# Hybrid attention block on one NeuronCore: buffers that TensorE reads begin at multiples of 128 bytes, and the last two down-projections of half the row tiles share one accumulation

## Chip, cores and metric

The kernel runs on one core of one Trainium2 chip. The metric is the device time of one execution in microseconds (us); lower is better. Everything is float32, and the large matrix products are made from three products each of rounded parts (below).

## What is computed

One layer over x of 1024 rows by 1024 columns. The reference, cut to what matters here:

```
h   = rms_norm(x, g_pre_mix)
proj = h @ w_in                              # 1024 x 2824
mix = concat(gated_delta_rule(...), sliding_window_attention(...)) @ w_out
x   = x + rms_norm(mix, g_post_mix)
h   = rms_norm(x, g_pre_ffn)
u   = causal_depthwise_conv(h @ w_up, ffn_conv_w) + ffn_conv_b   # 1024 x 5632
gate, val = split(u, 2)
y   = (gelu(gate) * val) @ w_down            # contraction over 2816
out = x + rms_norm(y, g_post_ffn)
```

## The kernel before

Three stages run one after the other. The **input projection** (0 to 300 us) multiplies row tiles of 128 by the columns of w_in. The **mixer** (to about 605 us) does the delta rule, the attention and the output projection tile by tile. The **channel block** (`ffn_block`, from 605 us to the end) does the up- and down-projection.

**Products.** A float32 operand is kept as two rounded parts, hi and lo, and a product is three matmuls that accumulate in one PSUM bank: hi by hi, hi by lo, lo by hi. These three are called a triple here. Each matmul has a stationary operand of 128 x 128, loaded before it, and a moving one of 128 x 512. Lines 2256 to 2258 are the triple of the up-projection (stationary `f_w_hi`, `f_w_lo`; moving `split`), lines 2274 to 2276 that of the down-projection (stationary `f_y_hi`, `y_lo`; moving `f_w_hi`, `f_w_lo`), 176 to 178 that of the input projection's convolved columns (stationary `slab_w`, moving `split`), 622 to 624 that of its other columns (stationary `p_tile_hi`, `p_tile_lo`; moving `slab_w` for the first group of columns, 8 triples in each of 8 row tiles, then `p_group`), 1777 to 1779 that of the output projection (stationary `m_mix_hi`, `m_mix_lo`; moving `split`).

**Channel block.** The 2816 hidden columns are taken in FG = 11 groups of 256. A step g does the up-projection of group g (4 channel blocks of 128, 16 triples each) and then the down-projection of group g - 1, whose results go to all 8 row tiles, two banks of 512 columns each: 16 banks, two triples each. Four PSUM banks (`sums`) take turns, and VectorE adds each full bank to the running sum `acc` in `h_t` (line 2139). After the last step `down(FG)` does the down-projection of the last group; its y parts lie in a free slot of `f_w_hi` and `f_w_lo`. TensorE may start a bank once the bank of four before it has been added (`s_acc`), and may start `down(FG)` once the low parts of the last y are there (`s_ylo`, line 2151).

**Last y.** For each of two channel blocks: ScalarE's first tap (L2058) and VectorE's two others (L2127), the product with the gelu (L2161, `s_prod`), ScalarE's rounding (L2090, `s_yhi`), VectorE's low part (L2151, `s_ylo`). On VectorE they stand between additions, in an order written out by hand.

**Tail.** For each row tile t: after its two additions ScalarE squares it (L2113), VectorE scales the sum (L2224), GpSimd raises it to -0.5 (L2240), VectorE multiplies by it and the gain (L2174), the residual is added (L1983; on GpSimd for tiles 0 to 5, on VectorE for 6 and 7), and the tile is stored (L2047). VectorE's order is: additions of tile t, then L2174 of tile t - 1, then L2224 of tile t.

**Where buffers begin.** Buffers of a core's memory are handed out one after another, so the start of each is the sum of the sizes before it. Offsets of the starts from a multiple of 128 bytes, before and after the change:

| buffer | role | before | after |
|---|---|---|---|
| `slab_w`, `split`, `stage`, `y_lo` | both | 0 | 0 |
| `table`, `exact`, `p_tile_hi`, `p_tile_lo`, `p_group` | both | 64 | 0 |
| `f_w_hi`, `f_w_lo`, `f_y_hi` | both | 64 | 0 |
| `m_mix_hi`, `m_mix_lo` | stationary | 96 | 0 |

The 64 comes from `conv_taps`, 48 float32 or 192 bytes in each partition. The slices that the triples of the table take are whole multiples of 512 bytes apart, except in `p_group`'s third part.

Of the kernel before, what the change touches and what calls it, by code (L numbers as in the profile page):

```python
# [20 lines left out]
P = 128  # L21
# [3 lines left out]
ALU = mybir.AluOpType  # L25
# [4 lines left out]
D = 1024  # L30
S = 1024
T = S // P
KD = D // P
HALF = 512
# [5 lines left out]
GTAPS, FTAPS = 4, 3  # L40
DFF = 2816
A_CH = 3 * GH * DK
A_TILES = A_CH // P
# [47 lines left out]
NG = 7  # L91
# [4 lines left out]
class Kept:  # L96


    def __init__(self, nc, ctx):
        sb = lambda name, shape, dt=F32: ctx.enter_context(nc.sbuf_tensor(name, shape, dt))  # L100
        sem = lambda name: ctx.enter_context(nc.semaphore(name))

        def under(name, shape, dt=F32):
            with nc.sbuf_tensor(name, shape, dt) as m:
                return m

        self.slab_w = under("slab_w", [P, KD * S], F32R)
        self.h_t = sb("h_t", [P, KD, S])
        self.split = sb("split", [P, 2, KD, S], F32R)
        self.stage = sb("stage", [P, 2, 2 * P * KD])  # L110
        self.x = sb("x_tile", [P, D])
        self.y_lo = under("y_lo", [P, 2, S], F32R)
        self.conv = sb("conv", [P, 2, S])
        self.g_post, self.g_ffn = self.conv[:, 0], self.conv[:, 1]
        self.taps = sb("conv_taps", [P, GTAPS * A_TILES])
        self.g_out = under("g_out", [P, D])
        self.table = sb("table", [P, T_ROPE])
        self.exact = sb("exact", [P, 4, P], F32R)
        self.gates = sb("gates", [P, T, NG, GH])
        self.own_rows = sb("own_rows", [P, T, GH])  # L120
        self.cum_rows = sb("cum_rows", [P, P], F32R)
        self.sums = ctx.enter_context(nc.psum_tensor("sums", [P, 4, HALF], F32))
        self.s_stage = [sem(f"s_stage{n}") for n in range(2)]
        self.s_slab = [sem(f"s_slab{n}") for n in range(2)]
        self.s_qkv_out = [sem(f"s_qkv_out{n}") for n in range(2)]
        self.s_whi, self.s_wlo = sem("s_whi"), sem("s_wlo")
        self.s_pair, self.s_first, self.s_tap = sem("s_pair"), sem("s_first"), sem("s_tap")
        self.s_conv, self.s_silu = sem("s_conv"), sem("s_silu")
# [95 lines left out]
def project(nc, io, kept):  # L224

    SLOTS = 4
    H = GH
    with ExitStack() as ctx:  # L228
        sb = lambda name, shape, dt=F32: ctx.enter_context(nc.sbuf_tensor("p_" + name, shape, dt))
# [19 lines left out]
        power = sb("power", [P, 1])  # L249
# [11 lines left out]
        ps_t = ctx.enter_context(nc.psum_tensor("ps_t", [P, 2, HALF], F32))  # L261
# [8 lines left out]
        s_whi, s_wlo = kept.s_whi, kept.s_wlo  # L270
        s_taps = sem("s_taps")
# [218 lines left out]
        def _(dve):  # L490
# [46 lines left out]
            for c in range(NCH):  # L537
                g, k0, nk = CHUNKS[c]
# [19 lines left out]
            sums = gate_sums.rearrange("p (c t h) -> p c t h", c=2, h=H)  # L558

            dve.wait_ge(s_ps_g, 1)  # L560
            dve.tensor_copy(kept.taps[:], ps_t[:, 0, 0:GTAPS * A_TILES]).then_inc(s_taps, 1)
            dve.wait_ge(s_taps, 1)
            split_lo(dve, kept, 1)
            conv_rest(dve, kept, 0, 0)
# [113 lines left out]
def mix_block(nc, io, kept):  # L678
    project(nc, io, kept)

    with ExitStack() as ctx:
        sb = lambda name, shape, dt=F32: ctx.enter_context(nc.sbuf_tensor("m_" + name, shape, dt))
# [12 lines left out]
        zw = [m.rearrange("p (h c) -> p h c", c=P) for m in (left[:, A_TILES * P:(A_TILES + H) * P], late_zw[:])]  # L695
        row = right[:, 0:ROW]
        o = right[:, ROW:ROW + H * P].rearrange("p (h c) -> p h c", c=P)
        gs = sb("gs", [P, 2, NG, H])
        power = sb("power", [P, 2, H])

        gates, own_rows, cum_rows, exact = kept.gates, kept.own_rows, kept.cum_rows, kept.exact
        row_cum = sb("row_cum", [P, H, P], F32R)

        norm2 = sb("norm2", [P, 2, 2, 2 * H])
        k_pow = sb("k_pow", [P, 2, H])
        k_gate = sb("k_gate", [P, 2, 3, H])
        K_RN, K_LOW, K_NEG = range(3)
        k_out = sb("k_out", [P, 2, H, P])
        b_v = sb("b_v", [P, H, P])
# [9 lines left out]
        resid = sb("resid", [P, H, P])  # L719
        v_new = sb("v_new", [P, H, P])  # L720
        squares = v_new
        o_stat = sb("o_stat", [P, 5, H])
        norm_w = sb("norm_w", [P, P])
        junk = sb("junk", [P, H, P], BF16)

        NB = P // BASE
        SKEW = BASE * (BASE + 1)
        blk = sb("blk", [H * NB, SKEW])
        products = sb("products", [H * NB, (BASE // 2) ** 3])
        half_sum = sb("half_sum", [H * NB, (BASE // 2) ** 2])  # L730

# [3 lines left out]
        v_b = sb("v_b", [P, 2, 2, KVH * HD])  # L735
        probs = sb("probs", [P, PAIRS, P])
        p_t = sb("p_t", [P, PAIRS, P])
        sinks = sb("sinks", [P, PAIRS])
        neg_sinks = sb("neg_sinks", [P, PAIRS])
        c_stat = sb("c_stat", [P, 6, 2 * PAIRS])  # L740

        mix_a = sb("mix_a", [P, H * P])
        mix_c = sb("mix_c", [P, 2, D - H * P])
        mix_hi = sb("mix_hi", [P, KD, P], F32R)
        mix_lo = sb("mix_lo", [P, KD, P], F32R)
        d_stat = sb("d_stat", [P, 6])
        y = sb("y", [P, D])
        table = kept.table
        tab = lambda at: table[:, at:at + P]
        ident = tab(T_ID)  # L750
# [1131 lines left out]
FG = FT // 2  # L1882


def ffn_block(nc, io, kept):
# [4 lines left out]
    with ExitStack() as ctx:  # L1890
# [54 lines left out]
        def n_down(g):  # L1945
            return 3 * g + 2

        LAST_DOWN = n_down(FG) - 2

        def steps(eng, step):  # L1950
            with eng.Fori(1, FG - 1) as g:
# [6 lines left out]
        def dn_w(part, kind):  # L1958
            return (w_hi, w_lo)[part][:, kind].rearrange("p (k n) -> p k n", k=2)

        def y_of(part, last):
            if last:
                return (w_hi, w_lo)[part][:, VALUE].rearrange("p (c s) -> p c s", c=2)
            return (y_hi, y_lo)[part][:]
# [86 lines left out]
        def _(act):  # L2051
# [57 lines left out]
            step(0, False, lead=True)  # L2109
            steps(act, step)  # L2110
            for t in range(T):
                act.wait_ge(s_acc, 16 * (FG - 1) + 2 * t + 2 + 4)
                act.activation(junk[:], acc[:, t], ACT.Square, accum_out=stat[:, 0, t:t + 1]).then_inc(s_sq, 1)  # L2113

        @block.vector
        def _(dve):
# [19 lines left out]
            def accumulate(m, t, half):  # L2136
                dve.wait_ge(s_dn, m + 2)
                cols = acc[:, t, half * HALF:(half + 1) * HALF]
                dve.tensor_tensor(cols, ps_dn[:, (2 * t + half) % 4], cols, ALU.add).then_inc(s_acc, 1)  # L2139

            def step(g, last, lead=False):
                if not lead:
                    split(n_down(g), DOWN, 0)
                for c in range(2):
                    convolve(4 * g + c, c, g * 2 + c)
                split(LAST_DOWN if last else n_gate(g + 1), GATE, 0)
                for c in range(2):
                    convolve(4 * g + 2 + c, 2 + c, g * 2 + (c + FT))
                def low_part(c):
                    dve.wait_ge(s_yhi, 2 * g + c + 1)  # L2150
                    dve.tensor_tensor(y_of(1, last)[:, c], conv[:, 2 + c], y_of(0, last)[:, c].bitcast(F32), ALU.subtract).then_inc(  # L2151
                        s_ylo, 1)

                for j in range(2 * T):
                    if not lead:
                        accumulate(g * 16 + (j - 16), j // 2, j % 2)
                    if j in (3, 6):
                        c = (j - 3) // 3
                        dve.wait_ge(s_gelu, 2 * g + c + 1)
                        dve.wait_ge(s_conv, 4 * g + c + 5)  # L2160
                        dve.tensor_tensor(conv[:, 2 + c], conv[:, c], conv[:, 2 + c], ALU.mult).then_inc(s_prod, 1)  # L2161
                    if j == 9 and not last:
                        split(n_value(g + 1), VALUE, 1)
                    if j in (9, 12) and last:
                        low_part((j - 9) // 3)
                if not last:
                    for c in range(2):
                        low_part(c)

            def finish(t):  # L2170
                if t == T - 1:
# [44 lines left out]
            for t in range(T + 1):  # L2216
                if t < T:
                    for half in range(2):
                        accumulate(16 * (FG - 1) + 2 * t + half, t, half)
                if t >= 1:  # L2220
                    finish(t - 1)
                if t < T:
                    dve.wait_ge(s_sq, t + 1)
                    dve.tensor_scalar(stat[:, 1, t:t + 1], stat[:, 0, t:t + 1], 1.0 / D, EPS, ALU.mult, ALU.add).then_inc(s_ms, 1)  # L2224
# [20 lines left out]
        def _(pe):  # L2245
# [13 lines left out]
                if 1 in halves:  # L2259
                    op.then_inc(s_pair, 1)  # L2260

            def down(g):
                last = isinstance(g, int) and g == FG
                kind = GATE if last else DOWN
                pe.wait_ge(s_wlo, LAST_DOWN if last else n_down(g))
                pe.wait_ge(s_ylo, 2 * g)
                for j in range(2 * T):
                    t, half = j // 2, j % 2
                    pe.wait_ge(s_acc, g * 16 + (j - 15))
                    for k in range(2):  # L2270
                        y = slice(t * P, (t + 1) * P)
                        cols = slice(half * HALF, (half + 1) * HALF)
                        bank = ps_dn[:, j % 4]
                        pe.matmul(bank, y_of(0, last)[:, k, y], dn_w(0, kind)[:, k, cols], start=(k == 0), stop=False)  # L2274
                        pe.matmul(bank, y_of(0, last)[:, k, y], dn_w(1, kind)[:, k, cols], start=False, stop=False)  # L2275
                        op = pe.matmul(bank, y_of(1, last)[:, k, y], dn_w(0, kind)[:, k, cols], start=False, stop=(k == 1))  # L2276
                    op.then_inc(s_dn, 1)

            def ups(g):
                for kind, n in ((GATE, n_gate(g)), (VALUE, n_value(g))):  # L2280
# [3 lines left out]

            def step(g, last):
                ups(g)
                down(g)

            pe.sem_inc(s_dn, 1)
            pe.wait_ge(s_rows, 48)  # L2290
# [16 lines left out]
            for c in range(2):  # L2307
                up(2 + c, VALUE, c)
            steps(pe, step)
            down(FG)  # L2310


# [29 lines left out]
```

## Time and profile before

| | |
|---|---|
| time, 3 runs | 1361.29 us median, 1359.57 to 1361.96 |
| profiled execution | 1361.83 us, span 1360.0 us |
| TensorE busy | 1278.4 us, 94% |
| VectorE, ScalarE, GpSimd busy | 52%, 30%, 11% |
| granted TensorE clock, mean | 0.972 |

The span is what the instruction records cover; the time of an execution is a little longer. A matmul's row has the time from its start until its results are out, and the next one starts before that, so the pace of TensorE is read from the starts of rows.

### The profile page before, as it was taken

What the parts mean: (1) busy time and instruction counts of PE and PEld (TensorE: products, weight loads), DVE (VectorE), ACT (ScalarE), POOL (GpSimd) and SP (SyncE); (2) the same over time, 40 slices, a digit from 0 to 9 for tenths busy, and PEclk for the clock granted to TensorE, in tenths of its full rate; (3) what the DMA queues carried; (4) which work ended last, traced back from release to release, by engine and by line L of the source; (5) the groups of instructions that cost most, each with busy time, mean ns of one, the idle gap of its engine ahead of it and who ended that gap; (6) DMA issues with size and microseconds to landing.
All of it is one profiled execution on the core that took longest, in us unless ns stands there. A gap on an engine that the chain in (4) does not pass through costs nothing.

```text
span 1360.0 us, 17354 instructions
## 1 busy us (share of the span) xinstructions
PE 1278.4 (94%) x6360; PEld 1071.8 (79%) x6360; DVE 708.7 (52%) x1076; ACT 410.7 (30%) x754; POOL 148.7 (11%) x184
## 2 busy tenths in 40 slices
PE   5999999993999999979999999999999999999994
PEld 4888878883888888757888888888888888888883
DVE  5332444545666666536444545454535353636358
ACT  5221233643344455334221222212121213121212
POOL 1221001300233333112000000000000000000005
PEclk9999999995899999989999999999999999999998
DMA  7321323443333331122201010101011111110213
GB/s 249 118 90 52 92 84 98 147 162 112 89 101 94 102 102 58 50 95 93 93 32 62 31 62 31 62 31 62 32 60 50 42 62 38 55 61 1 90 65 124
DMA packets 90698, 106.52 MB, mean 78 GB/s; under 512 B 17407, under 2 KB 75551, under 8 KB 90655
## 3 DMA queue, kind: packets, MB, share of 16 engines
q1 hardware_dynamic: 90655, 105.96, 23.8%
q8 instruction: 26, 0.43, 0.1%
q14 instruction: 17, 0.14, 0.0%
HBM read 82.84 MB, written 23.10 MB: 78 GB/s over the span
## 4 chain that ended last, share of the span: by engine, by line
PE 52%; POOL 1%; DVE 1%; issue 1%; ACT 0%; POOLq 0%
PE f_ps_up L2258 12%; PE f_ps_up L2257 12%; PE f_ps_up L2256 12%; PE sums L2276 6%; PE sums L2275 6%; PE sums L2274 5%; POOL stage L1983 1%; POOL f_conv L1983 0%; DVE split L2181 0%; POOL f_stat L2240 0%; DVE f_w_lo L2122 0%; ACT f_w_hi L2054 0%; POOLq L1890 0%; DVE f_conv L2194 0%; DVE h_t L2174 0%
## 5 line engine op out<-in xcount | busy, mean ns | idle before, releaser
L2258 PE MATMUL f_ps_up<-split,f_w_lo 128*128 128x512 f32 x704 | 278.7, 396 | 0.0
L2256 PE MATMUL f_ps_up<-split,f_w_hi 128*128 128x512 f32 x704 | 275.1, 391 | 3.1 <-DVE split L2181 3.1
L2257 PE MATMUL f_ps_up<-split,f_w_hi 128*128 128x512 f32 x704 | 277.3, 394 | 0.0
L2127 DVE SCALAR_TENSOR_TENSOR f_conv<-f_ps_up,f_taps,f_conv 128x1023 f32<-128x1023 f32 x88 | 112.8, 1282 | 280.2 <-ACT f_conv L2058 274.8
L2256 PEld LDWEIGHTS f_ps_up<-split,f_w_hi 128*128 128x128 f32 x704 | 133.0, 189 | 33.7 <-DVE f_w_lo L2122 2.1
L2257 PEld LDWEIGHTS f_ps_up<-split,f_w_hi 128*128 128x128 f32 x704 | 133.0, 189 | 31.0
L2258 PEld LDWEIGHTS f_ps_up<-split,f_w_lo 128*128 128x128 f32 x704 | 133.2, 189 | 26.8
L2058 ACT ACTIVATE f_conv<-f_ps_up,f_taps 128x1024 f32<-128x1024 f32 x44 | 53.1, 1207 | 331.1 <-PE f_ps_up L2258 331.1
L2139 DVE TENSOR_TENSOR h_t<-sums,h_t 128x512 f32<-128x512 f32 x176 | 117.0, 685 | 40.7 <-PE sums L2276 40.0
L2276 PE MATMUL sums<-f_w_hi,y_lo 128*128 128x512 f32 x320 | 127.0, 397 | 0.0
L2275 PE MATMUL sums<-f_w_lo,f_y_hi 128*128 128x512 f32 x320 | 125.5, 392 | 0.0
L2274 PE MATMUL sums<-f_w_hi,f_y_hi 128*128 128x512 f32 x320 | 124.6, 390 | 0.0
L2122 DVE TENSOR_TENSOR f_w_lo<-stage,f_w_hi 128x2048 fp32r<-128x2048 f32 x33 | 75.5, 2288 | 49.1 <-ACT f_w_hi L2054 49.1
L2240 POOL TENSOR_TENSOR f_stat<-f_stat,f_power 128x1 f32<-128x1 f32 x8 | 5.4, 669 | 704.4 <-DVE f_stat L2224 704.4
L176 PE MATMUL sums<-split,slab_w 128*128 128x512 f32 x192 | 76.6, 399 | 0.5 <-PEq L228 0.5
L178 PE MATMUL sums<-split,slab_w 128*128 128x512 f32 x192 | 75.6, 394 | 0.0
L177 PE MATMUL sums<-split,slab_w 128*128 128x512 f32 x192 | 75.3, 392 | 0.0
L2090 ACT CAST f_y_hi<-f_conv 128x1024 fp32r<-128x1024 f32 x20 | 20.1, 1050 | 173.5 <-PE sums L2276 171.4
L2275 PEld LDWEIGHTS sums<-f_w_lo,f_y_hi 128*128 128x128 f32 x320 | 60.1, 188 | 15.1
L197 DVE SCALAR_TENSOR_TENSOR conv<-sums,conv_taps,conv 128x1023 f32<-128x1023 f32 (+6 forms) x39 | 46.8, 1199 | 47.0 <-ACT conv L188 46.0
L2274 PEld LDWEIGHTS sums<-f_w_hi,f_y_hi 128*128 128x128 f32 x320 | 60.1, 188 | 13.3
L2276 PEld LDWEIGHTS sums<-f_w_hi,y_lo 128*128 128x128 f32 x320 | 60.1, 188 | 13.1
(293 smaller groups left out, 2079.5 us busy)
## 6 DMA issues: line engine op xcount, KB each, us to landing
stage<-in_w_up SPq DMA_DIRECT2D x22, 1024.0 KB, 5.1
stage<-in_w_down SPq DMA_DIRECT2D x11, 1024.0 KB, 4.9
x_tile<-in_x SPq DMA_DIRECT2D x12, 512.0 KB, 4.3
stage<-in_w_in SPq DMA_DIRECT2D x6, 1024.0 KB, 6.6
qkv<-conv SPq DMA_DIRECT2D x11, 512.0 KB, 3.6
rows<-p_row SPq DMA_DIRECT2D x8, 644.0 KB, 3.2
stage<-rows SPq DMA_DIRECT2D x8, 644.0 KB, 4.4
stage<-in_w_in SPq DMA_DIRECT2D x8, 512.0 KB, 6.1
```

The lines of the kernel that those rows point to most:

```text
L176: pe.matmul(bank, w_hi, h_hi[:, k, cols], start=(k == 0), stop=False)
L177: pe.matmul(bank, w_hi, h_lo[:, k, cols], start=False, stop=False)
L178: op = pe.matmul(bank, w_lo, h_hi[:, k, cols], start=False, stop=(k == KD - 1))
L2122: dve.tensor_tensor(w_lo[:, kind], raw[:, slot], w_hi[:, kind].bitcast(F32), ALU.subtract).then_inc(s_wlo, 1)
L2127: op = dve.scalar_tensor_tensor(conv[:, q, k:S], ps_up[:, q % 2, 0:S - k], taps[:, bass.ds(ct + (FTAPS - 1 - k) * 2 * FT, 1)], conv[:, q, ...
L2139: dve.tensor_tensor(cols, ps_dn[:, (2 * t + half) % 4], cols, ALU.add).then_inc(s_acc, 1)
L2256: pe.matmul(bank, hi, h_hi[:, k, cols], start=(k == 0), stop=False)
L2257: pe.matmul(bank, hi, h_lo[:, k, cols], start=False, stop=False)
L2258: op = pe.matmul(bank, lo, h_hi[:, k, cols], start=False, stop=(k == KD - 1))
L2274: pe.matmul(bank, y_of(0, last)[:, k, y], dn_w(0, kind)[:, k, cols], start=(k == 0), stop=False)
L2275: pe.matmul(bank, y_of(0, last)[:, k, y], dn_w(1, kind)[:, k, cols], start=False, stop=False)
L2276: op = pe.matmul(bank, y_of(1, last)[:, k, y], dn_w(0, kind)[:, k, cols], start=False, stop=(k == 1))
```

## The change

It does two things. First, `conv_taps` is widened to 128 columns, of which 48 are used, and the mixer's small buffers that TensorE does not read are handed out last; so every buffer that TensorE reads begins at a multiple of 128 bytes. No instruction is added or removed by that. Second, for row tiles 4 to 7 the down-projection of group 9 (the last but one, y in `f_y_hi` and `y_lo`) is not done in the last step, but together with that of group 10: four triples accumulate in one bank, which is then added once. VectorE makes 8 additions fewer, TensorE the same number of matmuls. In the last step VectorE's work for the last y is moved forward between the 8 additions that are left.

```
-        self.taps = sb("conv_taps", [P, GTAPS * A_TILES])
+        self.taps = sb("conv_taps", [P, P])
...
-        gs = sb("gs", [P, 2, NG, H])
-        power = sb("power", [P, 2, H])
...
         mix_hi = sb("mix_hi", [P, KD, P], F32R)
         mix_lo = sb("mix_lo", [P, KD, P], F32R)
+        y = sb("y", [P, D])
+        gs = sb("gs", [P, 2, NG, H])
+        power = sb("power", [P, 2, H])
...
+        APART = T // 2
+        LAST_SUM = 16 * (FG - 2) + 2 * APART
...
+                if last:
+                    for j in range(2 * APART):
+                        accumulate(g * 16 + (j - 16), j // 2, j % 2)
+                        if j < 2:
+                            product(j)
+                        if j in (3, 5):
+                            low_part((j - 3) // 2)
+                    return
...
-                        accumulate(16 * (FG - 1) + 2 * t + half, t, half)
+                        accumulate(LAST_SUM + 2 * t + half, t, half)
...
+            def down_bank(m, parts, t, half):
+                y, cols = slice(t * P, (t + 1) * P), slice(half * HALF, (half + 1) * HALF)
+                bank = ps_dn[:, (2 * t + half) % 4]
+                pe.wait_ge(s_acc, m + 1)
+                for n, (last, kind, k) in enumerate(parts):
+                    pe.matmul(bank, y_of(0, last)[:, k, y], dn_w(0, kind)[:, k, cols], start=(n == 0), stop=False)
+                    pe.matmul(bank, y_of(0, last)[:, k, y], dn_w(1, kind)[:, k, cols], start=False, stop=False)
+                    op = pe.matmul(bank, y_of(1, last)[:, k, y], dn_w(0, kind)[:, k, cols], start=False, stop=(n == len(parts) - 1))
+                op.then_inc(s_dn, 1)
+
+            before, final = ([(last, kind, k) for k in range(2)] for last, kind in ((False, DOWN), (True, GATE)))
+
+            def down(g, last):
+                pe.wait_ge(s_wlo, n_down(g))
+                pe.wait_ge(s_ylo, 2 * g)
+                for j in range(2 * (APART if last else T)):
+                    down_bank(g * 16 + (j - 16), before, j // 2, j % 2)
+
+            def down_last():
+                pe.wait_ge(s_wlo, LAST_DOWN)
+                pe.wait_ge(s_ylo, 2 * FG)
                 for j in range(2 * T):
-                    t, half = j // 2, j % 2
...
+                    down_bank(LAST_SUM + j, final if j < 2 * APART else before + final, j // 2, j % 2)
```

On VectorE, in the last step, after the taps of the last channel blocks, there stood before (L2139 is an addition, L2161 a product, L2151 a low part, L2224 the first tile's scaled sum):

```order
L2139 TENSOR_TENSOR h_t<-sums,h_t 128x512 x4
L2161 TENSOR_TENSOR f_conv<-f_conv 128x1024
L2139 TENSOR_TENSOR h_t<-sums,h_t 128x512 x3
L2161 TENSOR_TENSOR f_conv<-f_conv 128x1024
L2139 TENSOR_TENSOR h_t<-sums,h_t 128x512 x3
L2151 TENSOR_TENSOR f_w_lo<-f_conv,f_w_hi 128x1024
L2139 TENSOR_TENSOR h_t<-sums,h_t 128x512 x3
L2151 TENSOR_TENSOR f_w_lo<-f_conv,f_w_hi 128x1024
L2139 TENSOR_TENSOR h_t<-sums,h_t 128x512 x5
L2224 TENSOR_SCALAR f_stat<-f_stat 128x1
```

and in the same place of the changed program, where an addition is L2141, a product L2159, a low part L2153 and the scaled sum L2233:

```order
L2141 TENSOR_TENSOR h_t<-sums,h_t 128x512
L2159 TENSOR_TENSOR f_conv<-f_conv 128x1024
L2141 TENSOR_TENSOR h_t<-sums,h_t 128x512
L2159 TENSOR_TENSOR f_conv<-f_conv 128x1024
L2141 TENSOR_TENSOR h_t<-sums,h_t 128x512 x2
L2153 TENSOR_TENSOR f_w_lo<-f_conv,f_w_hi 128x1024
L2141 TENSOR_TENSOR h_t<-sums,h_t 128x512 x2
L2153 TENSOR_TENSOR f_w_lo<-f_conv,f_w_hi 128x1024
L2141 TENSOR_TENSOR h_t<-sums,h_t 128x512 x4
L2233 TENSOR_SCALAR f_stat<-f_stat 128x1
```

The two products moved ahead of 3 and 5 additions, and the second low part stands behind 6 additions instead of 13.

On TensorE, a row tile's bank in the last part of the program (tiles 4 to 7) held only the last group's triples before, with both operands in `f_w_hi` and `f_w_lo`:

```order
L2274 MATMUL sums<-f_w_hi 128x512
L2275 MATMUL sums<-f_w_lo,f_w_hi 128x512
L2276 MATMUL sums<-f_w_hi,f_w_lo 128x512
L2274 MATMUL sums<-f_w_hi 128x512
L2275 MATMUL sums<-f_w_lo,f_w_hi 128x512
L2276 MATMUL sums<-f_w_hi,f_w_lo 128x512
```

and holds now the triples of both groups, the last but one first:

```order
L2276 MATMUL sums<-f_w_hi,f_y_hi 128x512
L2277 MATMUL sums<-f_w_lo,f_y_hi 128x512
L2278 MATMUL sums<-f_w_hi,y_lo 128x512
L2276 MATMUL sums<-f_w_hi,f_y_hi 128x512
L2277 MATMUL sums<-f_w_lo,f_y_hi 128x512
L2278 MATMUL sums<-f_w_hi,y_lo 128x512
L2276 MATMUL sums<-f_w_hi 128x512
L2277 MATMUL sums<-f_w_lo,f_w_hi 128x512
L2278 MATMUL sums<-f_w_hi,f_w_lo 128x512
L2276 MATMUL sums<-f_w_hi 128x512
L2277 MATMUL sums<-f_w_lo,f_w_hi 128x512
L2278 MATMUL sums<-f_w_hi,f_w_lo 128x512
```

So the 16 triples of group 9 for tiles 4 to 7 moved from ahead of the last down-projection to its second half.

## Rows read from the trace of the kernel before

**Rows 1.** The page: busy us, share of the span and instructions of each engine.

```profile
PE 1278.4 (94%) x6360; PEld 1071.8 (79%) x6360; DVE 708.7 (52%) x1076; ACT 410.7 (30%) x754; POOL 148.7 (11%) x184
```

**Rows 2.** Busy time by stretch: us, then busy us and instructions by engine, granted clock.

```profile
620.00:1298.00 678.00, 678.00 (x2958) 554.71 (x2957) 325.11 (x310) 154.05 (x120) 6.95 (x1) 1.00 0.15 50
```

**Rows 3.** Groups of instructions: up-, down- and output projection, with counts.

```profile
L2256 PE MATMUL f_ps_up<-split,f_w_hi 128*128 128x512 f32 x704 | 275.1, 391 | 3.1 <-DVE split L2181 3.1
...
L2274 PE MATMUL sums<-f_w_hi,f_y_hi 128*128 128x512 f32 x320 | 124.6, 390 | 0.0
...
L1777 PE MATMUL sums<-split,m_mix_hi 128*128 128x512 f32 x128 | 54.6, 426 | 1.5 <-DVE m_mix_lo L1464 1.5
```

**Rows 4.** TensorE's timeline: start, us; of each kind two triples' first matmuls.

```profile
50.41 0.40 PE L622 MATMUL sums<-slab_w,p_tile_hi 128*128 128x512 f32 x1
...
53.91 0.40 PE L622 MATMUL sums<-slab_w,p_tile_hi 128*128 128x512 f32 x1
...
199.81 0.39 PE L176 MATMUL sums<-split,slab_w 128*128 128x512 f32 x1
...
221.57 0.39 PE L176 MATMUL sums<-split,slab_w 128*128 128x512 f32 x1
...
598.57 0.39 PE L1777 MATMUL sums<-split,m_mix_hi 128*128 128x512 f32 x1
...
601.38 0.40 PE L1777 MATMUL sums<-split,m_mix_hi 128*128 128x512 f32 x1
...
1276.86 0.39 PE L2256 MATMUL f_ps_up<-split,f_w_hi 128*128 128x512 f32 x1
...
1290.59 0.39 PE L2256 MATMUL f_ps_up<-split,f_w_hi 128*128 128x512 f32 x1
...
1302.30 0.39 PE L2274 MATMUL sums<-f_w_hi,f_y_hi 128*128 128x512 f32 x1
...
1319.64 0.39 PE L2274 MATMUL sums<-f_w_hi,f_y_hi 128*128 128x512 f32 x1
...
1321.02 0.39 PE L2274 MATMUL sums<-f_w_hi 128*128 128x512 f32 x1
...
1335.30 0.39 PE L2274 MATMUL sums<-f_w_hi 128*128 128x512 f32 x1
```

**Rows 5.** Timeline of the tail, VectorE, GpSimd and TensorE.

```profile
1326.59 1.27 DVE L2174 SCALAR_TENSOR_TENSOR h_t<-h_t,f_stat,g_out 128x1024 f32<-128x1024 f32 x1
...
1336.25 1.27 DVE L2139 TENSOR_TENSOR h_t<-sums,h_t 128x512 f32<-128x512 f32 x2
1337.44 2.97 DVE L2174 SCALAR_TENSOR_TENSOR h_t<-h_t,f_stat,g_out 128x1024 f32<-128x1024 f32 x1
...
1340.40 1.27 DVE L2139 TENSOR_TENSOR h_t<-sums,h_t 128x512 f32<-128x512 f32 x2
...
1336.92 2.41 POOL L1983 TENSOR_TENSOR stage<-stage,h_t 128x1024 f32<-128x1024 f32 x1
...
1343.76 0.39 PE L2276 MATMUL sums<-f_w_hi,f_w_lo 128*128 128x512 f32 x1
...
1349.94 1.06 ACT L2113 ACTIVATE x_tile<-h_t 128x1024 f32<-128x1024 f32 x1 [2.94 <-DVE h_t L2139]
...
1352.67 0.14 DVE L2224 TENSOR_SCALAR f_stat<-f_stat 128x1 f32<-128x1 f32 x1
```

**Rows 6.** Timeline of the last y: VectorE and ScalarE.

```profile
1299.59 2.60 DVE L2127 SCALAR_TENSOR_TENSOR f_conv<-f_ps_up,f_taps,f_conv 128x1023 f32<-128x1023 f32 x2 [8.33 <-ACT f_conv L2058]
1302.10 2.48 DVE L2139 TENSOR_TENSOR h_t<-sums,h_t 128x512 f32<-128x512 f32 x4
1304.50 1.21 DVE L2161 TENSOR_TENSOR f_conv<-f_conv 128x1024 f32<-128x1024 f32 x1
...
1312.82 1.22 DVE L2151 TENSOR_TENSOR f_w_lo<-f_conv,f_w_hi 128x1024 fp32r<-128x1024 f32 x1
...
1305.74 1.05 ACT L2090 CAST f_w_hi<-f_conv 128x1024 fp32r<-128x1024 f32 x1 [6.19 <-DVE f_conv L2161]
```

More of the change, by code:

```diff
@@ L560, in _ @@
             dve.wait_ge(s_ps_g, 1)
-            dve.tensor_copy(kept.taps[:], ps_t[:, 0, 0:GTAPS * A_TILES]).then_inc(s_taps, 1)
+            dve.tensor_copy(kept.taps[:, 0:GTAPS * A_TILES], ps_t[:, 0, 0:GTAPS * A_TILES]).then_inc(s_taps, 1)
             dve.wait_ge(s_taps, 1)
@@ L697, in mix_block @@
         o = right[:, ROW:ROW + H * P].rearrange("p (h c) -> p h c", c=P)
-        gs = sb("gs", [P, 2, NG, H])
-        power = sb("power", [P, 2, H])
         gates, own_rows, cum_rows, exact = kept.gates, kept.own_rows, kept.cum_rows, kept.exact
         row_cum = sb("row_cum", [P, H, P], F32R)
-        norm2 = sb("norm2", [P, 2, 2, 2 * H])
-        k_pow = sb("k_pow", [P, 2, H])
-        k_gate = sb("k_gate", [P, 2, 3, H])
         K_RN, K_LOW, K_NEG = range(3)
@@ L721, in mix_block @@
         squares = v_new
-        o_stat = sb("o_stat", [P, 5, H])
         norm_w = sb("norm_w", [P, P])
@@ L727, in mix_block @@
         SKEW = BASE * (BASE + 1)
-        blk = sb("blk", [H * NB, SKEW])
         products = sb("products", [H * NB, (BASE // 2) ** 3])
@@ L737, in mix_block @@
         p_t = sb("p_t", [P, PAIRS, P])
-        sinks = sb("sinks", [P, PAIRS])
-        neg_sinks = sb("neg_sinks", [P, PAIRS])
-        c_stat = sb("c_stat", [P, 6, 2 * PAIRS])
         mix_a = sb("mix_a", [P, H * P])
@@ L745, in mix_block @@
         mix_lo = sb("mix_lo", [P, KD, P], F32R)
+        y = sb("y", [P, D])
+        gs = sb("gs", [P, 2, NG, H])
+        power = sb("power", [P, 2, H])
+        norm2 = sb("norm2", [P, 2, 2, 2 * H])
+        k_pow = sb("k_pow", [P, 2, H])
+        k_gate = sb("k_gate", [P, 2, 3, H])
+        o_stat = sb("o_stat", [P, 5, H])
+        blk = sb("blk", [H * NB, SKEW])
+        sinks = sb("sinks", [P, PAIRS])
+        neg_sinks = sb("neg_sinks", [P, PAIRS])
+        c_stat = sb("c_stat", [P, 6, 2 * PAIRS])
         d_stat = sb("d_stat", [P, 6])
-        y = sb("y", [P, D])
         table = kept.table
@@ L2111, in _ @@
             for t in range(T):
-                act.wait_ge(s_acc, 16 * (FG - 1) + 2 * t + 2 + 4)
+                act.wait_ge(s_acc, LAST_SUM + 2 * t + 2 + 4)
                 act.activation(junk[:], acc[:, t], ACT.Square, accum_out=stat[:, 0, t:t + 1]).then_inc(s_sq, 1)
@@ L2152, in low_part, with product @@
                         s_ylo, 1)
+                def product(c):
+                    dve.wait_ge(s_gelu, 2 * g + c + 1)
+                    dve.wait_ge(s_conv, 4 * g + c + 5)
+                    dve.tensor_tensor(conv[:, 2 + c], conv[:, c], conv[:, 2 + c], ALU.mult).then_inc(s_prod, 1)
+                if last:
[6 more added lines that the diff above has]
+                    return
                 for j in range(2 * T):
@@ L2157, in step @@
                     if j in (3, 6):
[L2158 to L2162, printed above, removed]
-                        split(n_value(g + 1), VALUE, 1)
[L2164 to L2168, printed above, removed]
+                        product((j - 3) // 3)
+                    if j == 9:
+                        split(n_value(g + 1), VALUE, 1)
+                for c in range(2):
+                    low_part(c)
             def finish(t):
@@ L2260, in up @@
                     op.then_inc(s_pair, 1)
[L2262 to L2265, printed above, removed]
-                pe.wait_ge(s_ylo, 2 * g)
-                for j in range(2 * T):
-                    t, half = j // 2, j % 2
[L2269 to L2277, printed above, removed]
+            def down_bank(m, parts, t, half):
[10 more added lines that the diff above has]
+                pe.wait_ge(s_wlo, n_down(g))
+                pe.wait_ge(s_ylo, 2 * g)
+                for j in range(2 * (APART if last else T)):
[3 more added lines that the diff above has]
+                pe.wait_ge(s_ylo, 2 * FG)
+                for j in range(2 * T):
+                    down_bank(LAST_SUM + j, final if j < 2 * APART else before + final, j // 2, j % 2)
             def ups(g):
@@ L2286, in step @@
                 ups(g)
-                down(g)
+                down(g, last)
             pe.sem_inc(s_dn, 1)
@@ L2309, in _ @@
             steps(pe, step)
-            down(FG)
+            down_last()
 _INS = ["x", "g_pre_mix", "w_in", "gdn_conv_w", "gdn_A_log", "gdn_dt_bias", "gdn_norm_w", "attn_sinks", "w_out",
```

## The prediction

> **What bounds the kernel now.** I read the page first: TensorE is busy 94% of the span, VectorE 52% [rows 1]. In the channel block TensorE has no gap at all: from 620 to 1298 us it is busy 678.00 of 678.00 us at the full granted clock, 2.4 GHz, with 2958 matmuls, one per 229.2 ns [rows 2]. So whatever the pace of a matmul is, the block pays it. The pace is then read from the starts in TensorE's timeline, since one row's 0.39 us overlaps the next. Per triple [rows 4]:
>
> - input projection, `slab_w` with `split`, both at offset 0: 21.76 us over 32 triples, 0.680;
> - last down-projection, `f_w_hi`/`f_w_lo` with themselves, both at 64: 14.28 over 21, 0.680;
> - up-projection, stationary at 64, moving at 0: 13.73 over 20, 0.6865;
> - other down-projections, moving at 64, stationary at 64 (hi) and 0 (lo): 17.34 over 25, 0.6936;
> - input projection, stationary at 64, moving `slab_w` at 0: 3.50 over 5, 0.700;
> - output projection, stationary at 96, moving at 0: 2.81 over 4, 0.7025.
>
> The two kinds whose operands begin at the same offset run at 0.680, the four in which they differ are slower, each by an amount of its own. All are matmuls of one shape and data type at the full clock, and the difference is there in stretches in which the other engines do nearly nothing as well as beside them. That speaks for addresses, not for contention.
>
> In the tail another thing bounds. A row tile costs TensorE 4 triples, 2.72 us, but VectorE passes from one tile's additions to the next's in 4.15 us (1336.25 to 1340.40) [rows 5]. Of that 2.97 is the scaling L2174, which takes 1.27 where GpSimd is not adding a residual (2.41). TensorE starts its last matmul at 1343.76, but the scaled sum of the last tile comes at 1352.67 and the span ends 7.3 us later [rows 5]. So the end is set by VectorE and GpSimd working off a queue of row tiles.
>
> **The change, part by part.**
>
> *Alignment in the channel block.* After it stationary and moving operands all begin at offset 0, the state of the first kind, so I price every triple at 0.680. Up-projection: 704 triples [rows 3] x 0.0065 = 4.6 us. Down-projection: 320 triples at the slow pace [rows 3]; 32 belong to the last step and are counted with the tail; 288 x 0.0136 = 3.9 us. TensorE never waits there, so all of it should reach the end: 8.5 us. Nothing hides it. Bounds: nothing, if addresses are not the reason, and 8.5.
>
> A rule speaks against this. The Trainium skill, TensorE: Matmul & The Clock Gate, section Back-to-back issue gap, gives a warm matmul of N columns N / 2.4 + 2.5 ns whatever its addresses, 216 ns here, so the change would be worth nothing; by that rule a triple is 0.647 us everywhere. No row shows that: the best is 0.680 and the kinds differ by up to 0.0225, which an address-free rule can't give. I go by the rows.
>
> *Alignment in the input projection.* The first group of columns has 8 triples in each of 8 row tiles. In the first tile they wait for loads anyway; 56 x 0.020 = 1.1 us.
>
> *Alignment in the output projection.* 128 triples [rows 3] x 0.0225 = 2.9 us at most. But in the mixer these triples are fillers between serial steps of VectorE and ScalarE, and where TensorE then waits for them, a shorter filler only lengthens the wait. Between 0 and 2.9 I take 1.0, nearer to nothing. The small matmuls of the mixer are paced by their weight loads and are priced at nothing; the moved small buffers are read by VectorE, ScalarE and GpSimd only, and I see no row that prices their offsets: 0, with 1 us either way in the range.
>
> *The shared accumulation.* The number of triples from the start of the last step's down-projection on is the same, 16 x 2 x 2 = 64. Take 1298.1 as their start, and the old times up to there. VectorE: taps until 1302.19, then by durations of [rows 6] addition (0.62), product (to 1304.0), addition, product (to 1305.8), two additions (1307.1; ScalarE's second rounding ends at 1306.9), low part (1308.2), two additions (1309.5), low part: 1310.6. TensorE's first 16 triples end at 1298.1 + 10.9 = 1309.0. So a new wait of about 1.5 us arises ahead of `down_last`, which begins at 1310.6 and not at 1320.3. Queued behind it are all remaining matmuls, so it costs its full length on TensorE; the old one was covered by 32 triples. Then 48 triples: 1310.6 + 32.6 = 1343.3 for the last one, some 0.8 us earlier than now, no more.
>
> The gain is in who is late. Tiles 0 to 3 come at 2.72 us each and VectorE takes 4.15, so it falls behind as now, but 10 us earlier: its additions of tile 3 begin at about 1322.5 and those of tile 4 at 1326.7. Tiles 4 to 7 take TensorE 8 triples, 5.44 us, each, more than 4.15. By tile 6 VectorE waits for TensorE, and the last tile's addition starts right after its bank, at 1343.5. Then: addition 0.7, square and its accumulator 1.3, scaled sum at 1345.5. That is 1352.67 now [rows 5]: 7.2 us earlier. What follows is the same work in the same order (the power, the two residuals on VectorE, the store), 7.3 us. The residuals on GpSimd of tiles 4 and 5 must be done by then; at 5.44 us a tile they are.
> Bounds of this term: if TensorE's pace in it is 0.6936 and not 0.680, 48 triples cost 0.65 more and it is 6.5; each us by which the last y is later costs 1 us; and if the last residuals come beside each other without waiting it is 8.
>
> *Sum.* 4.6 + 3.9 + 1.1 + 1.0 + 7.2 = 17.8 us. The profiled span goes from 1360.0 to 1342.2, its execution from 1361.83 to 1344.0. The median of the runs is 0.54 below the profiled execution: **1343.5 us**.
>
> **Rivals.** A measurement of this kernel can tell about 0.2%, 2.7 us.
>
> - *Offsets are not the reason* for the pace, but, say, which banks of memory two buffers lie in, and these move by 320 bytes only. Then only the tail gains, 6.5: 1354.8. For it: the four slow kinds cost four different amounts, so the offset alone is not the whole story. Against it: two kinds of different buffers agree at 0.680, and both have equal offsets. Chance 0.08. The Trainium skill's rule named above comes to the same.
> - *Part of the pace is gained*, for instance because only low-order parts of the address matter and the up-projection keeps 0.6865: 4.6 less, 1348. The mixer giving nothing goes with it: up to 1349. Chance 0.10.
> - *The tail gives nothing.* The wait for the last y is longer than worked out, or the lock between VectorE and GpSimd falls worse. For it to eat 7 us, the last low part would have to come at 1317.8, later than VectorE's whole queue there lasts. Then 1350.7. Chance 0.06.
> - *Slower.* Equal offsets in all buffers make stationary and moving reads, or VectorE's writes, meet more often in the channel block, and a triple takes what the slow kind of the input projection takes, 0.700. Up: 704 x 0.0135 = 9.5 lost; down: 288 x 0.0064 = 1.8 lost; tail 48 x 0.020 = 1.0 less gain, so 6.2. Net 5.1 slower, 1366.4. It decides from a triple of about 0.694 on, where the loss of the up-projection, 5.3, with nothing gained in the down-projection comes near the tail's gain. Against it: 32 triples in a row at 0.680 with both at 0. Chance 0.04.
>
> **How the numbers follow.** My forecast has 0.70, with its own range 1340 to 1347: the mixer's term between 0 and 2.9 (2 us), the tail's between 6.5 and 8, and 1 us for the moved buffers and the run. 0.02 is left for less than 1339. The range 1339 to 1350 takes in the forecast and the partial case; above it lie the first, the third and the slower rival, 0.18. Faster by over 0.2%: all cases but the slower one and a remainder, 0.95; within 0.2%: 0.01; slower: 0.04.
>
> **What would show it.** In the changed profile: first matmuls of up-projection triples 0.680 apart, likewise down-projection; the same number of matmuls between 620 and 1290 in some 8 us less. In the last step a TensorE gap of 1 to 2 us ahead of the first matmul with both operands in `f_w_hi`, waited for from the low part L2153. VectorE's wait for TensorE before the additions of tiles 6 and 7, and L2183 at 1.3 us for tiles 5 and 6 instead of 3.0. The last matmul of TensorE and the end of the span 16 us apart now, would be about 10 apart. I am wrong if the triples stay at 0.6865 and 0.6936, if the gap is over 4 us, or if the clock falls after it.

## The result, and the profile after

The changed kernel takes 1342.66 us (median of 4 runs, 1337.75 to 1343.92) against 1360.59 us for the kernel before in the same comparison: ratio 0.9863, 95% interval 0.9846 to 0.9880. The forecast was 1343.5. The profiled execution took 1343.92 us with a span of 1341.9.

The page of the changed kernel answers to [rows 1]; the second row is the channel block's stretch by time (us, then busy us and instructions of TensorE, its weight loads, VectorE, ScalarE, GpSimd; then granted clock, DMA share and GB/s), which answers to [rows 2]:

```profile
span 1341.9 us, 17346 instructions
PE 1266.5 (94%) x6360; PEld 1071.1 (80%) x6360; DVE 698.5 (52%) x1068; ACT 411.1 (31%) x754; POOL 148.7 (11%) x184
...
620.00:1286.00 666.00, 666.00 (x2940) 551.48 (x2939) 322.53 (x307) 152.30 (x118) 6.96 (x1) 1.00 0.15 51
```

TensorE has no gap in the block now either, but a matmul starts every 226.5 ns (666.00 us / 2940) and not every 229.2. The starts in its timeline, as in [rows 4]:

```profile
47.64 0.40 PE L622 MATMUL sums<-slab_w,p_tile_hi 128*128 128x512 f32 x1
...
52.41 0.39 PE L622 MATMUL sums<-slab_w,p_tile_hi 128*128 128x512 f32 x1
...
1231.64 0.39 PE L2276 MATMUL sums<-f_w_hi,f_y_hi 128*128 128x512 f32 x1
...
1237.76 0.39 PE L2276 MATMUL sums<-f_w_hi,f_y_hi 128*128 128x512 f32 x1
...
1264.28 0.39 PE L2265 MATMUL f_ps_up<-split,f_w_hi 128*128 128x512 f32 x1
...
1277.88 0.39 PE L2265 MATMUL f_ps_up<-split,f_w_hi 128*128 128x512 f32 x1
```

The up-projection needs 13.60 us for 20 triples, 0.680 each (before 0.6865); the down-projection 6.12 for 9, 0.680 (before 0.6936); the input projection with `slab_w` moving 4.77 for 7, 0.681 (before 0.700).

The tail, TensorE's wait for the last y and then VectorE and GpSimd, as in [rows 5]:

```profile
1298.19 0.39 PE L2278 MATMUL sums<-f_w_hi,y_lo 128*128 128x512 f32 x1
1299.67 0.47 PE L2276 MATMUL sums<-f_w_hi 128*128 128x512 f32 x1 [1.09 <-issue]
...
1298.36 1.22 DVE L2153 TENSOR_TENSOR f_w_lo<-f_conv,f_w_hi 128x1024 fp32r<-128x1024 f32 x1
...
1311.55 1.27 DVE L2141 TENSOR_TENSOR h_t<-sums,h_t 128x512 f32<-128x512 f32 x2
1312.75 2.97 DVE L2183 SCALAR_TENSOR_TENSOR h_t<-h_t,f_stat,g_out 128x1024 f32<-128x1024 f32 x1
...
1327.19 0.69 DVE L2141 TENSOR_TENSOR h_t<-sums,h_t 128x512 f32<-128x512 f32 x1 [2.03 <-PE sums L2278]
1327.80 1.28 DVE L2183 SCALAR_TENSOR_TENSOR h_t<-h_t,f_stat,g_out 128x1024 f32<-128x1024 f32 x1
...
1332.63 0.69 DVE L2141 TENSOR_TENSOR h_t<-sums,h_t 128x512 f32<-128x512 f32 x1 [2.03 <-PE sums L2278]
1333.24 1.27 DVE L2183 SCALAR_TENSOR_TENSOR h_t<-h_t,f_stat,g_out 128x1024 f32<-128x1024 f32 x1
1334.54 0.15 DVE L2233 TENSOR_SCALAR f_stat<-f_stat 128x1 f32<-128x1 f32 x1
```

From 1298.19 to 1299.67 is one matmul (0.23) and a wait of 1.25 us that ends with the low part (1298.36 + 1.22). For the early tiles VectorE is still the slow one (scaling 2.97). At tiles 6 and 7 it waits 2.03 us for TensorE, the scaling beside no residual takes 1.28, and the last scaled sum comes 7.4 us before the end of the span, as before. TensorE's last matmul starts at 1332.2, 9.7 us before the end, where it was 16.2.

### The profile page after: what moved, and what is told of

The parts are those of the page before. It is cut to its first block, busy times and chain, and to the rows that moved or that the text cites. A ratio compares the mean times of both kernels' runs of the same rounds, so it can differ in the third digit from the quotient of the medians.

```text
span 1341.9 us, 17346 instructions
## 1 busy us (share of the span) xinstructions
PE 1266.5 (94%) x6360; PEld 1071.1 (80%) x6360; DVE 698.5 (52%) x1068; ACT 411.1 (31%) x754; POOL 148.7 (11%) x184
## 4 chain that ended last, share of the span: by engine, by line
PE 51%; POOL 1%; issue 1%; DVE 1%; ACT 0%; POOLq 0%
PE f_ps_up L2265 12%; PE f_ps_up L2266 12%; PE f_ps_up L2267 12%; PE sums L2276 5%; PE sums L2278 5%; PE sums L2277 5%; POOL stage L1985 1%; POOL f_conv L1985 0%; DVE split L2190 0%; POOL f_stat L2249 0%; DVE f_w_lo L2124 0%; ACT f_w_hi L2056 0%; POOLq L1890 0%; DVE f_conv L2203 0%; DVE h_t L2183 0%
## 5 line engine op out<-in xcount | busy, mean ns | idle before, releaser
L2267 PE MATMUL f_ps_up<-split,f_w_lo 128*128 128x512 f32 x704 | 275.1, 391 | 0.0
L2141 DVE TENSOR_TENSOR h_t<-sums,h_t 128x512 f32<-128x512 f32 x168 | 111.1, 686 | 39.8 <-PE sums L2278 39.7
```

Source lines behind the costliest of these rows:

```text
L2267: op = pe.matmul(bank, lo, h_hi[:, k, cols], start=False, stop=(k == KD - 1))
```

## The experiments

Stretches are read between the same points in each trace, in us: the first matmul of the first up-projection triple, the first matmul of the last one, and the end of the span.

| kernel | first up | last up | span | channel block | tail |
|---|---|---|---|---|---|
| before | 609.0 | 1297.5 | 1360.0 | 688.5 | 62.5 |
| changed | 607.2 | 1286.7 | 1341.9 | 679.5 | 55.2 |
| e1_align | 605.8 | 1285.6 | 1347.8 | 679.8 | 62.2 |
| e2_shared | 608.0 | 1295.6 | 1351.0 | 687.6 | 55.4 |

**e1_align, e2_shared: one part of the change each.** e1 is the kernel before with the buffers of the changed one, e2 the changed kernel with the buffers of before.

```
e1 (to the kernel before):
-        self.taps = sb("conv_taps", [P, GTAPS * A_TILES])
+        self.taps = sb("conv_taps", [P, P])          # and the mixer's small buffers last
e2 (to the changed kernel):
-        self.taps = sb("conv_taps", [P, P])
+        self.taps = sb("conv_taps", [P, GTAPS * A_TILES])   # and the small buffers where they were
```

> The kernel before with the alignment alone (wider conv_taps, the mixer's small buffers last); the order of work is that of before. My theory (the pace follows the offsets at which the two operands begin): triples of the channel block 0.680 us in both projections, the span about 11 us shorter than before (8.9 channel block, 2.3 input projection, mixer nothing), 1349 us; tail unchanged. Rival (the gain came from the shared accumulation and a shifted schedule): triples 0.6865 and 0.6936 as before, time within 3 us of before.

> The changed kernel with the buffers where they were before, so the shared accumulation alone. My theory: triples 0.6865 and about 0.6936 as before, a wait of 1 to 2 us ahead of the last y, the span 6.5 to 7 us shorter than before, about 1353 us, and the two single changes add up to the whole. Rival (the shared accumulation pays by itself nothing): within 2 us of before.

e1: 1349.13 us, ratio to the kernel before 0.9918 (0.9903 to 0.9933). e2: 1353.41 us, 0.9958 (0.9944 to 0.9972). The product of the two ratios is 0.9876, the whole change's 0.9863: they add up. Their stretches by time:

```profile
620.00:1285.00 665.00, 665.00 (x2936) 550.64 (x2935) 321.12 (x304) 151.33 (x117) 6.95 (x1) 1.00 0.15 51
```

```profile
620.00:1295.00 675.00, 675.00 (x2942) 552.16 (x2941) 324.14 (x308) 152.30 (x118) 6.95 (x1) 1.00 0.15 51
```

e1 has 226.5 ns a matmul and the tail of before, e2 229.4 ns and the tail of the changed kernel. So the alignment gives 8.7 us in the channel block beside the old order of work (before to e1) and 8.1 beside the new one (e2 to the changed kernel); the shared accumulation gives 7.1 us in the tail with the old buffers and 7.0 with the new. Neither needs the other, and both rivals are out.

**e3_all64, e4_split64: is it a multiple of 128, or an equal start?**

```
e3:     # Kept, ahead of slab_w and h_t
+        sb("pad", [P, 16])                                  # 64 bytes
e4:     # Kept, around split
+        sb("pad_a", [P, 16])
         self.split = sb("split", [P, 2, KD, S], F32R)
+        sb("pad_b", [P, 16])
```

> The changed kernel with 64 unused bytes ahead of all its buffers, so that every buffer begins at offset 64 of 128 and all offsets are still equal. Theory of equal offsets: all triples 0.680, time as the changed kernel, about 1342 us. Rival (each operand must begin at a multiple of 128, whatever the other does): triples slower than 0.680 everywhere, by 6 to 20 ns, and the input projection's convolved columns too, which were at 0.680 in both kernels; the time some 8 to 20 us longer.

> The changed kernel with only split moved by 64 bytes, so that in the up-projection the moving operand begins at 64 and the stationary at 0, the other way round than before. Theory of equal offsets: up-projection triples about 0.6865 again (or another slow value), the convolved columns of the input projection slow for the first time, 0.685 to 0.700, down-projection 0.680. Rival (only a stationary operand that begins off a multiple of 128 is slow): all of them 0.680. Span 1342 plus 5 to 10 by the first, 1342 by the second.

e3: 1341.90 us, 0.9867 (0.9850 to 0.9884), as fast as the changed kernel, though no buffer begins at a multiple of 128. Its stretch and two starts of the up-projection, 13.60 us over 20 triples:

```profile
620.00:1284.00 664.00, 664.00 (x2932) 549.79 (x2931) 320.06 (x302) 151.34 (x117) 6.29 (x1) 1.00 0.16 51
...
1262.22 0.39 PE L2266 MATMUL f_ps_up<-split,f_w_hi 128*128 128x512 f32 x1
...
1275.82 0.39 PE L2266 MATMUL f_ps_up<-split,f_w_hi 128*128 128x512 f32 x1
```

So an operand need not begin at a multiple of 128; the two must agree. e4, a single execution: 1360.55 us beside a median of 1359.53. Its rows, 20 triples each of the input projection's convolved columns (which never were slow) and of the up-projection:

```profile
204.77 0.39 PE L178 MATMUL sums<-split,slab_w 128*128 128x512 f32 x1
...
218.50 0.39 PE L178 MATMUL sums<-split,slab_w 128*128 128x512 f32 x1
...
1281.66 0.39 PE L2267 MATMUL f_ps_up<-split,f_w_hi 128*128 128x512 f32 x1
...
1295.66 0.39 PE L2267 MATMUL f_ps_up<-split,f_w_hi 128*128 128x512 f32 x1
```

0.6865 and 0.700: moving the moving operand is enough to slow both, the rival of the stationary operand is out. But 0.700 is more than the 0.6865 of before, and the span of 1358.5 is above the range that I gave. The two pads had a side effect that I had overlooked: together they move all buffers behind `split` by 128 bytes, so that the two operands of the up-projection lie 64 apart the other way round than before the change. In my theory that is nothing.

**e5_off32, e6_off96, e7_off128, e8_ylo64: how far must they agree?** In the first three only the length of `conv_taps` differs, so all buffers behind it move against `split`, `slab_w` and `y_lo`. e8 has 64 bytes ahead of `y_lo` and 64 behind it, and so again moves the rest by 128.

```
-        self.taps = sb("conv_taps", [P, P])
+        self.taps = sb("conv_taps", [P, P + 8])      # e5; + 24 in e6, + 32 in e7
e8:
+        sb("pad_a", [P, 16])
         self.y_lo = under("y_lo", [P, 2, S], F32R)
...
+        sb("pad_b", [P, 16])                         # behind conv, which lies on y_lo
```

> The changed kernel with conv_taps 32 bytes longer: every buffer behind it begins at offset 32 (before it was 64), split, slab_w and y_lo at 0. Theory of equal offsets: up-projection triples slower than 0.680, with the size of the loss open (0.683 to 0.700); down-projection slow around y_lo. Rival (64 is special, for instance a boundary of 64 bytes in what one read fetches): as slow as or slower than with 64. A tie to 32-byte reads would give 0.680.

> As the run with 32, with 96 bytes. If the loss grows with the part of a 128-byte line that lies behind the start, 96 differs from 32 and 64 lies between them; if only off or on a multiple of 128 counts, 32, 64 and 96 give the same pace, 0.6865 for the up-projection.

> As the run with 32, with 128 bytes: all buffers at multiples of 128 as in the changed kernel, but those behind conv_taps at another multiple within 256 and 512 than split and slab_w. If 128 is the length that counts: all triples 0.680, span as the changed kernel within 3 us. If the offsets must agree within 256 or 512: up-projection slower than 0.680, span 3 to 10 us longer.

> The changed kernel with y_lo alone (and the conv buffer that lies there) at offset 64. Theory of equal offsets: up-projection 0.680; down-projection triples slower by 0.006 to 0.014, all of it in the two matmuls around y_lo's load (the third matmul's start to the next first, 236 ns before). Rival (the down-projection's extra 13 ns came from y_hi and w at 64 and not from y_lo): 0.680.

A single execution each, 1364.75, 1366.31, 1360.73 and 1361.73 us beside one of 1361.41 for the kernel before: all four lose what the whole change had gained. The loss is in the channel block, 698.4, 701.2, 696.5 and 697.2 us against 679.5 in the changed kernel; their tails, 55.4 to 55.7, keep the gain. e7 refutes my theory in the form I had it. Every buffer in it that TensorE reads begins at a multiple of 128, and its up-projection takes 14.00 us for these 20 triples:

```profile
620.00:1303.00 683.00, 683.00 (x2938) 552.52 (x2937) 323.10 (x306) 151.42 (x118) 6.95 (x1) 1.00 0.15 50
...
1282.30 0.39 PE L2265 MATMUL f_ps_up<-split,f_w_hi 128*128 128x512 f32 x1
...
1296.30 0.39 PE L2265 MATMUL f_ps_up<-split,f_w_hi 128*128 128x512 f32 x1
```

232.5 ns a matmul over the whole stretch, more than before the change. It fits e4 and e8 too, whose buffers behind the pads had moved by the same 128: the up-projection of e8, with its operands 128 apart like those of e7, has the same pace. With 32, 64 and 96 bytes between them (e5, e4, e6) a triple takes 0.700, 0.700 and 0.703: the loss neither grows with the part of a line, nor is it the 0.6865 that I had given for all three, and 32 bytes are not free. e8 does not settle what it was made for. `y_lo` and `f_w_hi` differ by 64 in it (the other way round than before the change), and the down-projection took 0.693 as before, but e7 has the same 0.693 with the two 128 apart.

**e9_off256, e10_mix512: 256 or 512?**

```
e9:
-        self.taps = sb("conv_taps", [P, P])
+        self.taps = sb("conv_taps", [P, P // 2])     # 256 bytes instead of 512
e10:
+        sb("pad", [P, P // 2])                       # 256 bytes ahead of m_mix_hi
         mix_hi = sb("mix_hi", [P, KD, P], F32R)
```

> The changed kernel with conv_taps 256 bytes long instead of 512: every buffer still begins at a multiple of 128, and even the difference between the buffers behind conv_taps and split, slab_w and y_lo is a multiple of 256; only modulo 512 they differ. If the operands must agree modulo 256: all triples 0.680, time as the changed kernel, 1342 us. If modulo 512: up-projection about 0.690 (the output projection of the changed kernel, whose operands differ by 256, took 0.691), span some 8 to 13 us longer.

> The changed kernel with 256 unused bytes ahead of m_mix_hi, so that the output projection's operands, the last that differ, agree modulo 512 too. If 512 is the length: the output projection's undisturbed triples 0.680 instead of 0.691. Since they are fillers in the mixer I expect at most 0.5 us of the 1.4 us at the end; a gain that the times do not show. If the 0.691 came from other work beside it: no change of the triples.

e9: 1341.01 us, 0.9854 (0.9838 to 0.9871). Its `f_w_hi` and `split` agree modulo 256 and differ modulo 512, and 20 triples take 13.60 us:

```profile
620.00:1283.00 663.00, 663.00 (x2926) 549.17 (x2926) 319.10 (x302) 151.39 (x117) 5.35 (x1) 1.00 0.16 52
...
1261.97 0.39 PE L2265 MATMUL f_ps_up<-split,f_w_hi 128*128 128x512 f32 x1
...
1275.57 0.39 PE L2265 MATMUL f_ps_up<-split,f_w_hi 128*128 128x512 f32 x1
```

e10: 1341.02 us, 0.9856 (0.9840 to 0.9873), no different from e9 or the changed kernel; the output projection's triples stayed at a median of 0.692, as in the changed kernel (0.691), where their operands agree modulo 256 already. The fastest tenth of them take 0.680 in both; what slows the others, other work beside them for instance, was not tested.

All kernels together, mean time of a triple in us, from the start of its first matmul to that of the next triple, without the few over 0.75:

| start of stationary less moving, modulo 256 | triple | seen in |
|---|---|---|
| 0 | 0.680 | up-projection in 7 kernels, down-projection in 8 |
| 32 | 0.700 | up (e5) |
| 64 | 0.700 | up (e4) |
| 96 | 0.703 | up (e6) |
| 128 | 0.700 | up (e7, e8) |
| 192 | 0.687 | up (before, e2), `slab_w` as stationary (e4) |

At 128 the triples alternate between 0.696 and 0.704. The input projection's kinds with equal starts have a median of 0.680 to 0.684 in every kernel. Its first group (`slab_w` moving) is in line at 32, 96 and 128 (means of 0.700 in e5, 0.703 in e6, 0.697 in e4, e7 and e8), but not at 192, where its median is 0.700, before and in e2. The output projection, whose triples vary even at 0 (above), is left out. Offsets that are no multiple of 32 were not tried.

**e_apart2, e_apart6: the tail.**

```
-        APART = T // 2
+        APART = 2        # e_apart2, low parts at j = 2 and 3; 6 in e_apart6
```

> The changed kernel with 2 instead of 4 row tiles kept apart: the last step's down-projection has 4 banks, and tiles 2 to 7 share the accumulation; the second low part stands directly behind the first. My theory (the end is TensorE's last matmul plus about 10 us, and the wait for the last y costs its full length): TensorE waits 5.5 to 6 us for the last y instead of 1.3, ends 4.5 us later, span 4 to 5 us longer than the changed kernel, more if the granted clock falls in the wait. Rival (VectorE's queue still sets the end): the same time.

> The changed kernel with 6 row tiles kept apart, tiles 6 and 7 shared. My theory: no wait for the last y, TensorE ends 1.3 us earlier, but VectorE's queue of 4.15 us a tile sets the additions of tile 7 again, at about 3.7 to 4 us later than in the changed kernel: span 3 to 4.5 us longer. Rival (the wait for y is what is left to gain): span 1.3 us shorter.

e_apart2: 1347.18 us, 0.9916 (0.9898 to 0.9934), span 1345.5, its tail 61.1 us against 55.2. TensorE in and behind the wait, then two stretches by time, the granted clock third from the end:

```profile
1290.27 0.39 PE L2278 MATMUL sums<-f_w_hi,y_lo 128*128 128x512 f32 x1
1296.13 0.77 PE L2276 MATMUL sums<-f_w_hi 128*128 128x512 f32 x1 [5.47 <-issue]
...
1297.55 0.63 PE L2276 MATMUL sums<-f_w_hi 128*128 128x512 f32 x1
1297.97 0.63 PE L2277 MATMUL sums<-f_w_lo,f_w_hi 128*128 128x512 f32 x1
...
1296.00:1300.00 4.00, 3.87 (x10) 3.08 (x11) 0.72 (x2) 0.00 (x0) 0.00 (x0) 0.52 0.73 264
1300.00:1336.00 36.00, 36.00 (x160) 29.64 (x158) 17.81 (x27) 8.05 (x14) 17.99 (x13) 1.00 0.26 102
```

The wait is 5.6 us, 4.4 more than in the changed kernel. Behind it the clock adds to that: the granted clock is half (0.52 from 1296 to 1300), 1.2 GHz, for 3.5 us, and the matmuls start 0.43 apart instead of 0.23 (the first 0.56), some 1.6 us lost. The tail is 6.0 us longer, the sum of the two. So the wait for the last y costs its full length, as the forecast had it.

e_apart6: 1342.30 us, 0.9874 (0.9857 to 0.9892), span 1341.0, tail 56.9 us.

```profile
1325.52 1.27 DVE L2141 TENSOR_TENSOR h_t<-sums,h_t 128x512 f32<-128x512 f32 x2
...
1329.67 1.27 DVE L2141 TENSOR_TENSOR h_t<-sums,h_t 128x512 f32<-128x512 f32 x2
1330.87 2.90 DVE L2183 SCALAR_TENSOR_TENSOR h_t<-h_t,f_stat,g_out 128x1024 f32<-128x1024 f32 x1
```

Counted from the last up-projection triple, TensorE's last matmul starts 0.9 us earlier and not 1.3, and VectorE's queue of 4.15 us a tile does set the end, without a wait for TensorE. The cost in the tail is 1.7 us and not 3.7 to 4. Tile 7's additions come only some 0.2 us later than in the changed kernel; nearly all of the rest is tile 6's scaling, 2.90 beside GpSimd instead of 1.27. Why I had put the additions so much later was not settled; one row tile too many in the queue would be 4.15. The times don't tell this kernel from the changed one.

## Why the prediction was right, and where not

- **Who bounds what.** Right. The channel block paid the pace in full, the tail was VectorE's queue; e1 and e2 separate the two.
- **Channel block, 8.5 us.** Measured 9.0 for the whole change, and 8.7 and 8.1 for the alignment alone. The triples came at 0.680.
- **The reason.** Half right. That the two operands' starts must agree, and not each begin at a multiple, was shown by e3. "The same offset from a multiple of 128" has the wrong length: e7 has it and is slow, e9 differs by 256 and is fast. Among 128, 256 and 512 the length is 256. That the changed kernel had it right was luck, from the actual sum of its sizes: the buffers that TensorE reads all begin 128 past a multiple of 256. With 128 bytes more in `conv_taps`, which the prediction would have priced the same, the gain would have been gone (e7). In the trace of before nothing tells 128 and 256 apart, since both fast kinds agree in either. Why two kinds that are both 192 apart modulo 256 cost 0.6865 and 0.700 stays open, and so does what in the chip makes the two reads meet; the runs show which offsets are slow, not the mechanism.
- **The rule of the Trainium skill, TensorE: Matmul & The Clock Gate, section Back-to-back issue gap**, has a gap that depends on the columns alone. The formula that the prediction took from it, 216 ns, is given there for an isolated matmul; for a stream of weight loads and matmuls of 512 columns it has about 131 ns. Neither was seen here: 226.7 ns a matmul where the starts agree and up to 234, a third of the slowest triple, where they don't, at the same granted clock.
- **Input projection and mixer, 1.1 and 1.0 us.** The first up-projection triple starts 1.8 us earlier in the changed kernel, 2.1 were forecast; with 9.0 and 7.3 that makes the 18.1 us between the spans. But this pair of profiles doesn't measure the two terms: the convolved columns begin 2.3 us earlier (137.6 to 135.3), and from there to the up-projection it takes 0.5 more (471.4 to 471.9). All profiles together say more. In the seven kernels whose starts agree modulo 256 the convolved columns begin at 135.6 on average (134.7 to 136.7) and the rest takes 469.3 (468.1 to 471.9); in the six others, e4 left out because its convolved columns are slow, 136.9 (135.7 to 138.2) and 470.9 (469.2 to 472.0). These differences, 1.3 and 1.6 us, are of the forecast's size, but the groups overlap and each kernel has one profile, so they are suggested and not shown. So is the account that in the mixer a shorter filler mostly lengthens a wait: the output projection's rows add up to 2.3 us less (105.1 to 102.8).
- **Tail, 7.2 us.** Measured 7.3 for the whole change, and 7.1 and 7.0 for the shared accumulation alone. The wait for the last y was given as 1.5 us; it is 1.25, with another 0.1 earlier at a bank. VectorE's waits at tiles 6 and 7 and the shorter scalings are there as written.
- **Slower, by 5.1.** Did not happen, but e4 to e8 are near that case: with a triple at 0.700 to 0.703 in the up-projection they give back the tail's gain, and e5 and e6 some 3 to 5 us more. The cause is the opposite of the one given for this rival, unequal starts and not equal ones.

## What to carry to other kernels

Where TensorE is the bound and loads weights before every matmul, read the start-to-start time of equal matmuls for each pair of buffers; if pairs differ at the same clock, compare where stationary and moving operands begin, modulo 256 bytes here, and not only each one's own alignment. One buffer of odd length early in memory moves everything behind it, so put such buffers last. In a tail where another engine works off a queue of tiles, let TensorE produce the last tiles more slowly and the first ones sooner.

## What the runs showed of the hardware that I had not expected

A pair of operands that both begin at multiples of 128 bytes, but 128 apart modulo 256, costs 233 ns a matmul in the up-projection against 226.7, as much as 32 or 64 apart; 96 apart costs 234, 192 apart 229, and 256 apart nothing. Behind a wait of 5.6 us the granted clock was 1.2 GHz for 3.5 us of work, while it stayed at 2.4 behind one of 1.25 us.
